# Four outputs at once by quads of the contraction in three projections, and norm sums put into a later slot

## The reference

```python
xn = rms_norm(h, pre_norm[0])
u, g = split(xn @ pool_w_in)                    # 2048 -> 2 x 4096, "pool_in"
pooled = windowed means of u - u                # windows 2, 4, 8, 16 by groups of 1024 channels
out = ((pooled @ w_group) * scale * silu(g)) @ pool_w_out
h = h + rms_norm(out, post_norm[0]);  h = h + (p[0] @ ple_w_proj[0]) * sigmoid(rms_norm(h) @ ple_w_gate[0])
xn = rms_norm(h, pre_norm[1])
q_lat, kv_lat, k_pe, g = split(xn @ mla_w_in)   # "mla_in", 14 outputs of 128 here, the last 12 of g later
q = rms_norm(q_lat) @ w_uq;  k, v = rms_norm(kv_lat) @ w_ukv     # "uq", "uk", "uv"
o = causal attention over 16 heads
out = (o * silu(g)) @ mla_w_out                 # "mla_out"
h = h + rms_norm(out, post_norm[1]);  then the gate of layer 1 ("proj1", "plegate1")
```

## Time and profile before

| | us |
|---|---|
| median of three runs | 2775.85 (2771.81 to 2786.06) |
| profiled execution | 2772.93 |
| its span | 2771.1 |
| PE (TensorE matmul) busy | 2683.1, 97% of the span |
| DVE (VectorE) busy | 2027.1, 73% |
| ACT (ScalarE) busy | 1420.2, 51% |
| DMA | 191 GB/s on average |

### The profile page before, as it was taken

How to read it: one execution, slowest core, us unless ns; L and a number is a source line. 1 busy time by engine, 2 the same in 40 slices (tenths; PEclk the granted TensorE clock), 3 DMA queues, 4 the chain that set the end, 5 groups by cost and what they waited for, 6 DMA issues and landing times.

```text
span 2771.1 us, 42123 instructions
## 1 busy us (share of the span) xinstructions
PE 2683.1 (97%) x15974; PEld 2335.6 (84%) x15974; DVE 2027.1 (73%) x3086; ACT 1420.2 (51%) x2000; POOL 0.2 (0%) x4
## 2 busy tenths in 40 slices
PE   7899999999999999999999999999999999999999
PEld 3568779998878888888888888889988988988887
DVE  6686796975898888886566777777654898556577
ACT  6443434444555555554445555554445654575564
POOL 0000000000000000000000000000000000000000
PEclk9999999999999999999999999999999999999999
DMA  8666676550745555555554555445555445433444
GB/s 339 228 254 270 248 271 238 215 189 31 281 173 184 195 182 193 186 193 181 194 194 164 184 190 186 179 169 182 186 188 191 166 157 180 170 140 108 170 159 145
DMA packets 108297, 530.26 MB, mean 191 GB/s; under 512 B 8288, under 2 KB 8832, under 8 KB 56336
## 3 DMA queue, kind: packets, MB, share of 16 engines
q1 hardware_dynamic: 105648, 515.93, 51.6%
q10 hardware_dynamic: 2528, 12.66, 1.3%
HBM read 526.46 MB, written 2.10 MB: 191 GB/s over the span
## 4 chain that ended last, share of the span: by engine, by line
PE 65%; DVE 8%; issue 3%; ACT 3%; ACTq 0%; DVEq 0%; DMA 0%
PE ps L2032 34%; PE ps L2033 17%; PE ps L2024 3%; PE ps L2025 3%; PE ps L2026 3%; DVE lo L1137 2%; ACT hi L521 1%; PE ps L2377 1%; DVE ws L1728 1%; PE ps L2581 1%; PE ps L2579 0%; PE ps L2382 0%; DVE R L1775 0%; DVE O L1773 0%; ACT L882 0%
## 5 line engine op out<-in xcount | busy, mean ns | idle before, releaser
L1137 DVE TENSOR_TENSOR lo<-raw,hi 128x1024 fp32r<-128x1024 f32 x700 | 842.1, 1222 | 444.7 <-ACT hi L521 441.2
L521 ACT ACTIVATE hi<-raw 128x1024 fp32r<-128x1024 f32 x700 | 730.1, 1056 | 581.0 <-PE ps L2033 524.6
L2032 PE MATMUL ps<-x,hi 128*128 128x512 f32 x1376 | 478.7, 392 | 4.3 <-DVE x L1591 4.3
L2033 PE MATMUL ps<-x,lo 128*128 128x256 f32 x1376 | 385.8, 280 | 0.0
L2032 PE MATMUL ps<-xp,hi 128*128 128x512 f32 x1024 | 364.2, 400 | 4.5 <-DVE lo L1137 2.7
L2032 PE MATMUL ps<-y,hi 128*128 128x512 f32 x1024 | 363.3, 400 | 3.6 <-DVE y L2002 3.6
L2032 PEld LDWEIGHTS ps<-x,hi 128*128 128x128 f32 x1376 | 258.0, 187 | 61.3 <-issue 3.1
L545 ACT ACTIVATE hi<-raw 128x1024 fp32r<-128x1024 f32 x162 | 167.2, 1054 | 257.5 <-PE ps L2026 108.4
L2033 PE MATMUL ps<-xp,lo 128*128 128x256 f32 x1024 | 288.0, 281 | 0.0
L2033 PE MATMUL ps<-y,lo 128*128 128x256 f32 x1024 | 287.9, 281 | 0.0
L1200 DVE TENSOR_TENSOR lo<-raw,hi 128x1024 fp32r<-128x1024 f32 x162 | 192.3, 1220 | 96.2 <-ACT hi L545 95.8
(11 more groups left out here) (385 smaller groups left out, 4998.0 us busy)
## 6 DMA issues: line engine op xcount, KB each, us to landing
raw<-in_weights SPq DMA_DIRECT2D x483, 1024.0 KB, 4.8
wlast<-in_weights ACTq DMA_DIRECT2D x8, 1024.0 KB, 4.8
xf<-in_xt SPq DMA_DIRECT2D x8, 512.0 KB, 9.6
raw<-in_weights SPq DMA_DIRECT2D x4, 768.0 KB, 4.3
R<-in_xt ACTq DMA_DIRECT2D x1, 2048.0 KB, 7.3
out<-R SPq DMA_DIRECT2D x1, 1024.0 KB, 8.5
maskn<-in_maskn ACTq DMA_DIRECT2D x1, 512.0 KB, 3.6
ptr<-in_pt ACTq DMA_DIRECT2D x2, 256.0 KB, 3.8
```

The source lines that it names most:

```text
L521: act.activation(HI[p % PAIR][:, c], RAW[p % RING][:, c], ACT.Copy).then_inc(hi_ready, 1)
L1137: dve.tensor_tensor(LO[p % PAIR][:, c], RAW[p % RING][:, c], HI[p % PAIR][:, c].bitcast(F32), ALU.subtract).then_inc(lo_ready, 1)
L2032: pe.matmul(o, h, pair[:, :, k, :], start=start, stop=False, **kw)
L2033: return pe.matmul(o[:, 0, :], l, pair[:, 0, k, :], start=False, stop=stop, **kw)
```

## The change

`pool_in`, `mla_in` and `mla_out` get their first four outputs by quads: slot q of four holds the blocks k = 4q to 4q+3 of four outputs, which stand in four banks at once and are all finished only in slot 3. The layout of the first four slots is done by the DMA's access pattern (QUADS). The evictions of these outputs, and so the order of `split` and eviction on ACT and DVE, move: four splits first, then the evictions. In `pool_in` the eight first outputs are then taken two per slot over four slots. Norm sums: `pool_in` in the third slot (q = 2) ahead of its block 2, `mla_in` in the second ahead of its block 8. In `uq`, `uk` and `uv` the two pairs of banks swap, the wait for all outputs of `mla_in` moves to block 12 of the first slot, and `lat_hi(1)` on ACT goes from output 10 to output 11.

```diff
+QUADS = ("pool_in", "plegate0", "mla_in", "mla_out", "plegate1")
-                elif kind in ("plegate0", "plegate1") and k < 4:
+                elif kind in QUADS and k < 4:
@@ ACT, pool_in
+            split("pool_in", 0, 0)
             root("np", rs[:, :], PS[1][:, 0:T], D, eps2[:, :])
             root("nf", rs1[:, :], PS[0][:, 0:T], D)
+            for r in range(1, 4):
+                split("pool_in", 0, r)
+            for u in range(4):
+                pool_taken(u // 2, 2 * (u % 2))
+                pool_taken(u // 2, 2 * (u % 2) + 1)
+                split("pool_in", 1, u)
+            with act.Fori(2, 16) as i:
                 for r in range(4):
                     split("pool_in", i, r)
+                    pool_taken(i, r)
@@ ACT, mla_in
+            split("mla_in", 0, 0)
             root("m", rs[:, :], PS[2][:, 0:T], D)
+            split("mla_in", 0, 1)
...
+            split("mla_in", 0, 2)
+            split("mla_in", 0, 3)
             for j in range(14):
-                split("mla_in", j // 4, j % 4)
+                if j >= 4:
+                    split("mla_in", j // 4, j % 4)
...
-                if j == 10:
+                if j == 11:
                     lat_hi(1)
@@ ACT, mla_out (DVE the same, with p_rest)
+            split("mla_out", 0, 0)
+            split("mla_out", 0, 1)
             p_operand(1, ptr1, pth1)
+            split("mla_out", 0, 2)
+            split("mla_out", 0, 3)
@@ DVE, pool_in
+            split("pool_in", 0, 0)
+            split("pool_in", 0, 1)
             dve.wait_ge(sem("ups_zeroed"), 1)
             recip("np", rs[:, :])
             recip("nf", rs1[:, :])
+            split("pool_in", 0, 2)
+            split("pool_in", 0, 3)
@@ PE
+            def by_quads(phase, banks, pair, ready, free=None, at=(), then=None):
+                for q in range(4):
+                    def product(n, h, l):
+                        a, k = n // 4, 4 * q + n % 4
+                        if a == 0:
+                            ready(k)
+                        if (q, n) == at:
+                            then()
+                        if free and q == 0 and n % 4 == 0:
+                            free(a)
+                        return mm2(banks[a], h, l, pair, k, k == 0, k == 15)
+                    slot(phase, 0, q, product)
...
+            by_quads("pool_in", (4, 5, 6, 7), halves_of(xp, KD), lambda k: pe.wait_ge(sem("operand_rest"), reached("x", "np", k + 1)),
+                     at=(2, 2), then=norm_sums)
+            (outputs 4 to 7 in banks 0 to 3; before the first of them a wait for root "nf")
...
+            by_quads("mla_in", [mla_bank(j) for j in range(4)], halves_of(xm, KD),
+                     lambda k: pe.wait_ge(sem("operand_rest"), reached("x", "m", k + 1)),
+                     lambda a: pe.wait_ge(evacuated, EVAC["mla_in"] - (0 if a == 3 else 1)),
+                     at=(1, 8), then=lambda: sum_squares("m", "steps"))
...
-            pe.wait_ge(sem("y3_x"), 16)
             pe.wait_ge(evacuated, EVAC["mla_out"])
+            by_quads("mla_out", (4, 5, 6, 7), halves_of(y3, KD), lambda k: pe.wait_ge(sem("y3_x"), k + 1))
```

More of the change, by code:

```diff
@@ L409, in build, with pool_bank, mla_bank, out_bank @@
         level_banks = ((4, 5), (6, 3))
-        mla_banks = (0, 1, 6, 7)
+        def pool_bank(i, r):
+            return r if isinstance(i, int) and i == 1 else 4 + r
+        def mla_bank(j):
+            return (5, 6, 7, 4)[j] if j < 4 else (0, 1, 6, 7)[j % 4]
+        def out_bank(u, r):
+            return 4 + r if isinstance(u, int) and u < 4 else r % 2
+        def quad_done(phase, u, i, r):
+            early = isinstance(u, int) and u < 4
+            return 2 * BASE[phase] + 7 + u // 2 if early else 2 * (where(phase, i, r) + 1)
         turned_banks = (7, 0, 1, 2)
@@ L867, in _, with pool_taken @@
                 down_squares(o)
+            split("pool_in", 0, 0)
             root("np", rs[:, :], PS[1][:, 0:T], D, eps2[:, :])
             root("nf", rs1[:, :], PS[0][:, 0:T], D)
-            with act.Fori(0, 16) as i:
+            def pool_taken(i, r):
+                u = 2 * i + r // 2
+                act.wait_ge(halves_used, quad_done("pool_in", 4 * i + r, i, r))
+                act.activation(blk(sg, u) if r % 2 else up[r // 2][:, 16:UPW], PS[pool_bank(i, r)][:, T:2 * T], ACT.Copy).then_inc(sem("right"), 1)
+                if r % 2:
+                    act.wait_ge(evacuated, EVAC["pool_in"] + (4 * i + (r + 1)))
+                    act.wait_ge(sem("pool_made"), u + 1)
+                    act.activation(blk(ph, u), pf[:, :], ACT.Copy).then_inc(sem("pool_hi"), 1)
+                    act.activation(blk(sg, u), blk(sg, u), ACT.Silu).then_inc(sem("sg_ready"), 1)
+            for r in range(1, 4):
[5 more added lines that the diff above has]
+            with act.Fori(2, 16) as i:
                 for r in range(4):
                     split("pool_in", i, r)
[L875 to L882, removed]
+                    pool_taken(i, r)
             for i, r in turns(act, 16):
@@ L1020, in mla_right @@
                 dst = blk(ql, j) if j < 8 else blk(kpr, j - 8) if j < 10 else blk(sg2, j - 10)
-                act.wait_ge(halves_used, 2 * (BASE["mla_in"] + j + 1))
-                act.activation(dst, PS[mla_banks[j % 4]][:, T:2 * T], ACT.Copy).then_inc(sem("right"), 1)
+                act.wait_ge(halves_used, quad_done("mla_in", j, j // 4, j % 4))
+                act.activation(dst, PS[mla_bank(j)][:, T:2 * T], ACT.Copy).then_inc(sem("right"), 1)
             def lat_hi(q):
@@ L1050, in _ @@
                     dst = blk(qn, 4 * s + 2 * b, 2) if s < 4 else blk(qraw, 2 * b, 2)
-                    ins = act.activation(dst, PS[2 * (s % 2) + b][:, :], ACT.Copy)
+                    ins = act.activation(dst, PS[2 - 2 * (s % 2) + b][:, :], ACT.Copy)
                 ins.then_inc(evacuated, 1)
@@ L1069, in _ @@
                 for b in range(2):
-                    ins = act.activation(blk(kn, 4 * s + 2 * b, 2), PS[2 * (s % 2) + b][:, :], ACT.Copy)
+                    ins = act.activation(blk(kn, 4 * s + 2 * b, 2), PS[2 - 2 * (s % 2) + b][:, :], ACT.Copy)
                 ins.then_inc(evacuated, 1)
@@ L1080, in _ @@
                 for t in range(2):
-                    ins = act.activation(v2[:, t * 2048 + s * 512:t * 2048 + (s + 1) * 512], PS[2 * (s % 2) + t][:, :], ACT.Copy)
+                    ins = act.activation(v2[:, t * 2048 + s * 512:t * 2048 + (s + 1) * 512], PS[2 - 2 * (s % 2) + t][:, :], ACT.Copy)
                 ins.then_inc(evacuated, 1)
@@ L1704, in _ @@
+            for u in range(4):
+                pool_taken(0, u // 2, 2 * (u % 2))
+                pool_taken(0, u // 2, 2 * (u % 2) + 1)
+                split("pool_in", 1, u)
             for g in range(4):
-                with dve.Fori(4 * g, 4 * g + 4) as i:
+                with dve.Fori(max(4 * g, 2), 4 * g + 4) as i:
                     for r in range(4):
                         split("pool_in", i, r)
[L1708 to L1735, removed]
@@ L1736, in _ @@
+                        pool_taken(g, i, r)
             dve.wait_ge(sem("sg_ready"), 32)
@@ L2003, in _ @@
             clear_ssq()
+            split("mla_out", 0, 0)
+            split("mla_out", 0, 1)
             p_rest(1, ptr1, pth1, ptl1)
+            split("mla_out", 0, 2)
+            split("mla_out", 0, 3)
             for u in range(16):
-                split("mla_out", u // RING, u % RING)
-                out_left(1, u, u % 2)
+                if u >= 4:
+                    split("mla_out", u // RING, u % RING)
+                out_left(1, u, out_bank(u, u % RING))
                 if u:
```

97 lines of the change are left out of this document (69 added, 28 removed).

## The result

The changed kernel took 2750.92 us (median of 4 runs, 2738.84 to 2753.73) beside 2779.82 for the kernel before (4 runs, 2771.81 to 2786.06): ratio 0.9889, 95% interval 0.9847 to 0.9932. In two later comparisons it took 2759.55 (12 runs) beside 2782.33, ratio 0.9927 (0.9903 to 0.995), and 2755.82 (6 runs) beside 2784.19, ratio 0.9887 (0.9854 to 0.9919). So it is faster, by 29, 23 and 28 us, or 1%. The forecast of 2757 lies among these times, but its gain of 17.6 us was some 10 too small; it came out near because the execution that the sum started from, 2772.93, was one of the quicker ones of the kernel before.

A forecast was written before the change was run, and what follows sets the result against it. PE, 97% busy, was taken as the bound, so only its waits and half clock count. Gains of 3.4 + 0.95 + 8.4 + 4.9 = 17.6 us took 2772.93 to 2755.3, set at 2757 for the median; 8-in-10 range 2748 to 2767.

The forecast's parts named there:

- A: Start of `pool_in`, slots 0 and 1 with two norm sums: 7.4 us lost, 3.4 of it to be gained.
- B1: Start of `mla_in`, slots 0 and 1 with one norm sum: 0.95 us gained, 2.8 wait left before slot 2.
- B2: `mla_in` slot 13 and the way to `uq`: both waits and the slow clock behind them go, 8.4 us gained.
- C: Attention to `mla_out`: start 3.25 us earlier and the slow clock behind it gone, 4.9 us gained.
- rival 2: The pace of a block shifts; the faster one over 54 slots of `pool_in` gives 6 us, 2751; chance 0.14.
- The burst: `pool_in`, output pairs taken one per slot: DVE-ACT round 7.1 us against PE's 5.65, waits 1.4 and 1.5.
- the cover of 0.1 and of 1.0: Spare time in us: `lo` of `mla_in` slot 13 moves 2.1 against 2.0 late; `uq` has 1.0 spare.
- the three edges: Starts of `pool_in` and `mla_out`, and `mla_in` through `uq`: 26.5 us lost in all, 1% of the time.
- Rival 3: The waits only move, since the DVE-ACT-DVE chain catches PE later: 5 us gained, 2769.5; chance 0.11.
- Rival 4: Slower: the clock falls in `pool_in`'s burst over eight banks, 11.7 us slower, 2786; chance 0.04.
- rival 1: The burst in `pool_in` and the clocks take their worst values: 10.5 us gained, 2764; chance 0.21.
- stretch B1: Slots 0 and 1 of `mla_in` before the change: 16.70 us, clock 1.00 with waits of at most 1.5.

The follow-up runs named there:

- loads put back: Changed kernel with a one-column Sqrt ahead of ACT's `pool_in` loop, so that it loads tables every turn again: 2761.97 us, ratio 0.9945.
- Silu ahead: Kernel before with a one-column Silu ahead of ACT's `pool_in` loop, no order changed: 2769.47 us, ratio 0.9966.
- the three orders: Changed kernel with splits moved earlier in `pool_in` and `mla_in` and `pool_in`'s norm sums at block 10: 2738.46 us, ratio 0.9841; later 2748.63, 0.9873.

## Why the prediction was right, and where it was not

| Step | predicted | measured | from |
|---|---|---|---|
| A | 3.4 | 3.9 | before less loads put back, equal pace |
| B1 and B2 | 9.35 | 10.2 | `mla_in` 8.6, `uq` 1.6 |
| C | 4.9 | 4.8 | attention 3.3, half rate 1.5 |
| table loads | none | 8.6 | Silu ahead, and loads put back |
| pace, this execution | rival 2 | 7.5 | `pool_in` 5.8, `mla_out` 1.7 |

Together 35.0; less 0.5 for the later start of `pool_in` and 0.3 more in `plegate1` that is 34.2 of the 34.3. Without the pace 27.5 are left, beside medians that differ by 28.9, 22.8 and 28.4. (Of the 8.6 in `mla_in` 0.4 is pace too: its mean block was 0.3492 before and 0.3475 after.)

**A held, and its terms nearly.** Slot 2's wait was to be 1.05 and was 1.05 (gap 1.40). The burst's circuit was to be 7.1; on DVE and ACT it took

```profile
1546.84 2.36 DVE L1175 TENSOR_TENSOR lo<-raw,hi 128x1024 fp32r<-128x1024 f32 x2 [0.83 <-ACT hi L538]
...
1553.65 2.36 DVE L1175 TENSOR_TENSOR lo<-raw,hi 128x1024 fp32r<-128x1024 f32 x2 [0.83 <-ACT hi L538]
```

6.81, with no load in it. The circuit being shorter, the waits at slots 8 and 9 were 0.7 and 1.15 instead of 1.4 and 1.5. The one load is in the first round, as I took it:

```profile
1536.90 0.42 ACT L898 ACTIVATE ph<-pf 128x256 fp32r<-128x256 f32 x1 [3.46 <-DVE sg L1754]
1537.34 1.28 ACT L899 ACT_TABLE_LOAD   x1
1538.63 0.42 ACT L899 ACTIVATE sg<-sg 128x256 f32<-128x256 f32 x1
```

Silu starts 1.29 behind the load's start. The Trainium skill, "ScalarE: Activation LUTs", What ACT_TABLE_LOAD costs, adds a drain of 1.38; here it does not show, and 3.4 was nearer than the 2.0 that it gave.

**B1 and B2 held.** A wait stayed before slot 2 (gap 2.88, so 2.5; 2.8 forecast) with half rate for three to four blocks, and it was the larger part of what was still to be had (the three orders took it). Slot 13 has a gap of 0.41 and `uq` none: the cover of 0.1 and of 1.0 held. With the latent's rounding put back, 2.2 returned.

**C held**: the start is 0.3 late, at full clock; undone it costs 5.3.

**What failed is a step that I never took.** Under "The burst" I wrote that from slot 10 on "a pair comes every two slots", and ahead of the parts that "the counts of matmuls, splits and evictions stay, so all is a matter of what comes late next". I looked at the state of ACT's table only within the burst, and left the loop behind it as it was. But the code that now stands ahead of the loop changes the table with which it is entered, and by that what the loop must load in every turn. The trace of before had two signs: 16 loads on L521, which is a split and needs no table of its own, and waits on `lo` in the earlier trace rows that I set aside as not lying at the three edges. Followed to their places, five of the seven lie before slots 54, 56, 58, 60 and 62.

**The rivals.** Rival 2's mechanism came true in the profiled execution and is none of the change's: the same program gave it back in the next two. Rival 3 fell, all three edges gave nearly all of their sum. Rival 4 fell: the clock was 1.00 over slots 3 to 9, with three waits of 0.7 to 1.2 among eight banks (1.40, 1.04 and 1.50 less 0.35). Of rival 1 nothing came. The evidence that the prediction held against rival 4, waits of 1.3 to 1.5 that left the clock at 1.00 in stretch B1, was one execution's: with the same waits of 1.5 the clock of that stretch was 0.80 in the kernel before with Silu ahead. So half rate at B1 is a term that comes in one execution and not in another, worth 1.0 us there.

My absolute number was helped by luck. I put half of the distance between the profiled execution and the median of three on the sum; the medians of more runs lie at 2779.8 to 2784.5, 7 to 12 above that execution, and cancelled the missing 10.

## What to carry to other kernels

When code is unrolled ahead of a loop, ask in what state the loop is then entered: one activation of the right function set, on a column that nobody reads, took 32 table loads out of a loop and gave 8.6 us, nearly half as much as the four reordered edges (18.9). A first group of outputs taken by parts of the contraction hides the late end of its operand. What else stands in that group must then move too: the norm sums to a later slot, when their input is ready, and the split of the next weights ahead of the long chain of other work on ACT and DVE. Compare two executions stage by stage, between waits and at equal pace; totals of single executions of one program differ here by more than such an edit gives.

## What the runs showed of the hardware

A block of a 512-column and a 256-column matmul takes 0.3467 or 0.3533 us at the same granted clock of 1.00, over whole stages (`up`: 480.05 or 489.11 us; `down`: 238.50 or 243.09), and it is different in executions of one and the same program. Most changes from one to the other fall at a wait or at the norm sums; in four executions `up` went from the fast to the slow pace within the first 4 us behind its last wait, with no wait beside the change. `mla_in` had the fast pace in its slots 6 to 12 in all twelve traces. Over the five long stages (3856 blocks) it is worth some 25 us by these two lengths of a block (an estimate), about the width of the kernel before's runs (2764.63 to 2791.76). What chooses it stays open.

The half clock behind a wait is not a fixed charge, and the length of the wait alone does not decide it. It came behind 2.4 us before slot 2 of `mla_in` (three blocks of 0.64 in one execution, four in the next) and behind 3.6 and 5.3. With the sums early it did not come behind 2.4 in the same stage; with the latent's rounding put back it did not come behind 2.1 at slot 13, where the kernel before had it behind 2.1. And behind two waits of 1.5 at the start of `mla_in` it came in one execution (clock 0.80 over the stretch) and not in another (1.00).
